# Weight-part buffers at eight offsets modulo 128 bytes, and activation parts of one stage 256 bytes apart

## What is computed

```python
def block(args):                       # peer_ffn, one block of tokens
    xb, ib, gb = args
    h = jax.nn.gelu(jnp.einsum('md,mkd->mk', xb, exp_u[ib]).astype(F32_2), approximate=False)
    coef = (gb * h).astype(xb.dtype)
    return jnp.einsum('mk,mkd->md', coef, exp_v[ib])
```

## The kernel before

| tensor | modulo 128 | modulo 1024 |
|---|---|---|
| `ring0` to `ring3`, `w_hi0` to `w_hi3`, `w_lo0` to `w_lo3` | 32 | 32 |
| `x_hi`, `x_lo` (every chunk of 256 columns) | 64 | 64 |
| `xn_hi`, `xn_lo`, `mixT_hi`, `mixT_lo`, `mixT1_*` | 64 | 448 |
| `mixT2_hi`, `mixT2_lo` | 32 | 672 |
| `mixT3_hi`, `mixT3_lo` | 64 | 576 |
| `hidden_hi`, `hidden_lo` (all four halves) | 64 | 832 |

## Time and profile before

### The profile page before, as it was taken

How to read it: one execution, slowest core, us unless ns; L and a number is a source line. 1 busy time by engine, 2 the same in 40 slices (tenths; PEclk the granted TensorE clock), 3 DMA queues, 4 the chain that set the end, 5 groups by cost and what they waited for, 6 DMA issues and landing times. The chain is left out here.

```text
span 2566.0 us, 62482 instructions
## 1 busy us (share of the span) xinstructions
PE 2430.2 (95%) x22900; PEld 2282.3 (89%) x22900; DVE 1673.7 (65%) x3915; ACT 1312.5 (51%) x2406; POOL 596.0 (23%) x494
## 2 busy tenths in 40 slices
PE   5998899999989999999999999879999999999998
PEld 3997667578978999999999999868999999999997
DVE  3032632636445966888998666665967888998665
ACT  3322643457345665555444554546665555445554
POOL 0335133157336930000000000637920000000000
PEclk9999999999999999999999999989999999999999
DMA  8554023034114554444444554424555444444552
GB/s 274 181 164 133 17 79 95 23 116 132 45 57 135 187 189 165 163 164 163 164 163 163 182 192 152 130 76 133 194 183 169 163 162 160 164 163 164 189 187 82
DMA packets 153876, 373.32 MB, mean 145 GB/s; under 512 B 8920, under 2 KB 102888, under 8 KB 137232
## 3 DMA queue, kind: packets, MB, share of 16 engines
q1 hardware_dynamic: 151232, 369.27, 42.9%
q10 hardware_dynamic: 2512, 2.24, 0.3%
HBM read 370.44 MB, written 1.05 MB: 145 GB/s over the span
## 5 line engine op out<-in xcount | busy, mean ns | idle before, releaser
L3012 ACT ACTIVATE w_hi<-ring 128x512 fp32r<-128x512 f32 x1024 | 643.1, 632 | 686.6 <-PE bank L3067 367.1
L3018 DVE TENSOR_TENSOR w_lo<-ring,w_hi 128x512 fp32r<-128x512 f32 x864 | 594.9, 691 | 310.2 <-ACT w_hi L3012 307.9
L3049 PE MATMUL bank<-x_hi,w_hi 128*128 128x256 f32 x2048 | 578.2, 282 | 3.8 <-DVE w_lo L3018 3.6
L3067 PE MATMUL bank<-hidden_hi,w_hi 128*128 128x256 f32 x2048 | 578.3, 282 | 0.0
L3067 PE MATMUL bank<-hidden_hi,w_lo 128*128 128x256 f32 x2048 | 574.3, 280 | 0.0
L3049 PE MATMUL bank<-x_hi,w_lo 128*128 128x256 f32 x2048 | 572.3, 279 | 0.0
L3049 PE MATMUL bank<-x_lo,w_hi 128*128 128x256 f32 x2048 | 571.9, 279 | 0.0
L3067 PE MATMUL bank<-hidden_lo,w_hi 128*128 128x256 f32 x2048 | 569.8, 278 | 0.0
L375 POOL TENSOR_TENSOR w_lo<-ring,w_hi 128x512 fp32r<-128x512 f32 (+3 forms) x260 | 337.0, 1313 | 653.5 <-ACT w_hi L366 645.2
L3049 PEld LDWEIGHTS bank<-x_hi,w_hi 128*128 128x128 f32 x2048 | 385.9, 188 | 4.8 <-ACT hidden L3142 4.0
L3049 PEld LDWEIGHTS bank<-x_lo,w_hi 128*128 128x128 f32 x2048 | 386.0, 188 | 0.0
(11 more groups left out here) (522 smaller groups left out, 4048.3 us busy)
## 6 DMA issues: line engine op xcount, KB each, us to landing
ring<-in_peer_uT SPq DMA_DIRECT2D x128, 1024.0 KB, 4.9
ring<-in_peer_v SPq DMA_DIRECT2D x128, 1024.0 KB, 4.8
ring<-in_even_w_in SPq DMA_DIRECT2D x26, 1024.0 KB, 5.6
ring<-in_ada_w SPq DMA_DIRECT2D x24, 1024.0 KB, 7.8
ring<-in_odd_w_in SPq DMA_DIRECT2D x12, 1024.0 KB, 5.4
ring<-in_even_w_out SPq DMA_DIRECT2D x8, 1024.0 KB, 5.4
ring<-in_odd_w_out SPq DMA_DIRECT2D x8, 1024.0 KB, 5.3
ring<-in_peer_w_q SPq DMA_DIRECT2D x8, 1024.0 KB, 5.2
```

Source lines behind the costliest of these rows:

```text
L3012: act.activation(k.hi[q][:, :], k.ring[slot][:, q * PART:q * PART + PART], ACT.Copy).then_inc(k.hi_ready, 1)
L3018: eng.tensor_tensor(k.lo[q][:, :], k.ring[slot][:, q * PART:q * PART + PART], k.hi[q][:, :].bitcast(F32), ALU.subtract).then_inc(k.lo_read ...
L3049: mm = pe.matmul(k.bank[s][:, j * T:j * T + T], a[q][:, w], b[:, cc, :], start=(cc == 0 and n == 0), stop=(cc == KC - 1 and n == 2))
L3067: mm = pe.matmul(out, a[q][:, w], b[:, j, :], start=first and cc % 2 == 0 and n == 0, stop=last and cc % 2 == 1 and n == 2, skip_group_che ...
```

## The change

The order of instructions and what each one waits for are the same on every engine; only addresses change. Each of the eight weight parts is now a view of 512 columns into a buffer of 768 (3072 bytes), and starts at an offset of its own. `hidden_hi` and `hidden_lo` get rows of 320 columns, of which 256 are used, and a spacer of 256 bytes ahead of them. The scratch for descriptors shrinks from 16384 to 1024 bytes, which makes room for this; no DMA of this kernel is issued from GpSimd.

```diff
+HI_AT, LO_AT = (0, 4, 2, 16), (20, 28, 6, 12)
...
-        self.hi = [self.sb(f"w_hi{i}", [P, PART], F32R) for i in range(PARTS)]
-        self.lo = [self.sb(f"w_lo{i}", [P, PART], F32R) for i in range(PARTS)]
+        self.hi = [self.sb(f"w_hi{i}", [P, PART + T], F32R)[:, HI_AT[i]:HI_AT[i] + PART] for i in range(PARTS)]
+        self.lo = [self.sb(f"w_lo{i}", [P, PART + T], F32R)[:, LO_AT[i]:LO_AT[i] + PART] for i in range(PARTS)]
...
-        self.hh = k.sb("hidden_hi", [P, 2, T], F32R)
-        self.hl = k.sb("hidden_lo", [P, 2, T], F32R)
+        k.sb("before_hidden_hi", [P, T // 4])
+        self.hh = k.sb("hidden_hi", [P, 2, T + T // 4], F32R)[:, :, 0:T]
+        self.hl = k.sb("hidden_lo", [P, 2, T + T // 4], F32R)[:, :, 0:T]
...
-    nc = bacc.Bacc("TRN2", target_bir_lowering=False, num_devices=1)
+    nc = bacc.Bacc("TRN2", target_bir_lowering=False, num_devices=1, dynamic_dma_scratch_size=1024)
```

## The result

The changed kernel takes 2576.87 us (median of 8, 2574.73 to 2579.49) against 2564.15 us for the kernel before in the same session (2560.69 to 2570.76): ratio 1.0045, 95% interval 1.0035 to 1.0055. It is slower by 11.5 us by the ratio (9 to 14 by the interval); the medians differ by 12.7. The profiled execution spans 2577.7 us, 11.7 more than before. The forecast was 8 us faster.

A forecast was written before the change was run, and what follows sets the result against it. TensorE's distance between matmul starts was taken as the bound. Excess over the floor, 5.1 + 0.8 + 4.5 + 2.6, summed to 13.0 us; 8 were taken, so 2561.7 − 8 = 2553.7 us, range 2546 to 2580.

The forecast's parts named there:

- What bounds the kernel: Whole kernel: TensorE is the bound, so the distance from one matmul's start to the next one's is what counts.
- Terms 1 and 2: All engines: no instruction, wait or DMA added, removed or moved; ScalarE's copies and VectorE's subtractions on shifted parts at no cost.
- The floor: TensorE: 116.67 ns per matmul is a property of a moving float32r operand of 256 columns at full clock, not a conflict.
- The rival under the floor: Experts: the 9% between bf16 and float32r is a conflict, the spread removes half, 49 us go: 2513; chance 0.05.
- The lock argument: Experts and tokens: eight relations break the slow pattern handed from matmul to matmul; down stage gains 5 us, tokens 2 to 3.
- Down stage: Experts' down stage: 4608 of 6144 matmuls run 1.1 ns over the floor; at most 5.1 us to win.
- Up stage: Experts' up stage: first layer at the floor; half of the second layer's gated matmuls may be 1.1 ns over, 0.8 us to win.
- the slower rival: Experts: new relations behave like the mixT rows, 118.6 ns, giving 2577 us, or 2599 at 120.0 ns for all; chance 0.30.
- First layer's tokens: First layer's token projections: 1344 matmuls at 120.0 ns, 4.5 us of excess, about half expected won, 2 to 3 us.
- The rival on the other side: Experts: giving up the old relation in seven of eight parts costs 17 us, less 2 for tokens: 2577 us; chance 0.30.
- The sign for the forecast: Down stage without gates: about 1545 matmuls in 180 us instead of 1531 would show the forecast right.
- the ports: TensorE: by the page's rule of separate ports the time would stay at 2562 us, within the nothing-measurable rival; chance 0.20.

The follow-up runs named there:

- the faster versions: The changed kernel with all parts at 96 bytes, 96 and 224 in turn, or 96, 224, 352 and 480, hidden activation as before: ratios 0.9845, 0.9812, 0.9809.
- the base run: The changed kernel with all eight part offsets at 0 and the hidden activation as before, keeping buffer pitch and small scratch: ratio 1.0001 to the kernel before.
- the kernel with the longer spacer: The kernel before with the spacer ahead of x_hi at 64 bytes instead of 32, moving every activation 32 bytes and no part: ratio 1.0012.

## Why the prediction was wrong, point by point

1. **What bounds the kernel** was right: the distance between TensorE's starts, nothing else. 11.3 of the 11.7 us of the loss are there, and TensorE's idle time did not change. The 39 to 49 us of the faster versions are there too, less 6 to 8 us by which TensorE's idle time grew (135.8 us before, 142 to 144 in them).
2. **Terms 1 and 2** (no instruction moves, ScalarE and VectorE at no cost) were right: 631 and 690 ns, and the base run at 1.0001.
3. **The floor** was the first step that failed. It was inferred from rows that all kept a relation other than 64. The 64-column loads and the 512 moving columns showed that a shorter or rarer load doesn't lower the distance; I took that as proof that the load has no part in it. The runs showed 113.3 ns with full loads at another relation. The rival under the floor, given 0.05, named a possible 49 us; 49 us came, but not from this change, which has no part in relation 64, and that the two numbers agree is luck. It took half of a 9% difference between bf16 and float32r, where the earlier trace rows give 7% (116.7 against 109.3 ns), so half of it would be 45 us.
4. **The lock argument** was the step that turned the sign: with eight relations the slow pattern would not survive, "because a matmul whose load is ready always runs at the floor". I held that a stretch hands its pattern on, and in the kernel before it does (one level per stretch). But a row of changing relations does not fall to the floor: the changed kernel has one level, 118.1 ns, in all 136 stretches, with no wait in them. Changing the relation inside a part doesn't free a row of its slow pattern; the run with high parts at 96 and low ones at 0 lost the low level by it. Nor does only a break change the level: with parts at 96 and 224 bytes in turn some rows dropped from 117.8 to 113.3 ns at a change of part. So the argument holds for those places, which share their relation modulo 128, and fails for the eight of this change.
5. **The terms.** Down stage: 5.1 us to win, 3.4 lost. Up stage: 0.8 to win, 7.4 lost. A stage that stands at the lowest distance of the trace has nothing to win and everything to lose, and the 8 us taken from the sum leave that side out; only the slower rival had it. First layer's tokens: 2 to 3 to win, 0.2 won.
6. **The rival on the other side** was right in place and sign, and near in size. It named the relation that was given up and its threshold (a mean over 117.6 ns; it became 118.1). It put the new relations at the mixT rows' 118.6, which was 0.5 too high: 17 us for the experts, and 10.8 came. It took 2 us off for the tokens that did not come. That its 2577 us is the median measured is luck in part: it stands on 2561.7 us for the kernel before, which had 2564.15 beside the changed one. Its mechanism, that giving up the relation costs, is borne out by the run with all parts at 64 bytes. A chance of 0.30 was too low for it: every row of the trace with another place was slower, and the forecast had no row of its own.
7. **The signs.** 1019 matmuls in 120 us of the up stage, fewer than 1031, was the sign of the slower rival. The sign for the forecast, about 1545 in the down window, seems met by the 1544 above, but only since small matmuls have slipped into the window. The gated slots did stop alternating, at 118.1 ns and not at the floor: that sign could not tell the two apart.
8. **On the ports**, the page "TensorE: Matmul & The Clock Gate" of the Trainium skill (section "Part 2: What happens when you issue a matmul") says that the weight load doesn't take read bandwidth from the running matmul. That sits badly with these runs of float32r operands: 113.3 to 123.4 ns in the down stage with nothing changed but the addresses of weight parts, which the experts' matmuls load and don't stream. They don't show that it is read bandwidth that is lost.

Open is what makes the levels: the runs show which there are, and that a break or, in one kernel, a change of part can bring another, not the mechanism inside the memory. The parts' new places are also where ScalarE and VectorE write. That these writes are needed for a new level is ruled out for one case: in the kernel with the longer spacer the parts stayed where they were, and its up stage has 113.3 ns, which the kernel before never had. Whether they have a share elsewhere was not tested. Open too is how the 118.1 ns of the changed kernel splits into relations (mean 117.9) and changes of relation within a part. By part it doesn't follow the mean at all: part 1 would have (2 × 117.6 + 118.7) / 3 = 118.0 ns and has 116.6, part 3 would have 118.3 and has 119.2.

## What to carry to other kernels

In this kernel, with back-to-back matmuls that each load new float32r weights, the place of the weight parts moved the distance between matmuls by up to 8% (113.3 against 123.3 ns). The start of the stationary operand relative to the moving one, modulo 128 bytes, was the first thing to look at, but not all of it: two kernels with relation 64 ran at 0.985 and 1.001 of the time. So try the multiples of 16 as one uniform shift, measure each, and only then spread anything. High and low parts of one buffer at different relations lost the gain in the one run that tried it; different buffers could differ by multiples of 128, and here that gained another 9 us. And a value that all rows of one layout share is no floor of the hardware: it may be the layout's.

## What was not expected of the hardware

- **Fixed levels.** A row of matmuls without a break runs at one of two or three exact distances (in the experts 113.3 or 117.8 ns at relation 64; 116.7 or 117.8 at 96), and a wait of 0.26 us can move it from one to the other. At offset 80 the level is itself a pattern: distances of about 117 and 130 ns in turn, mean 123.3.
- **GpSimd's subtraction is shorter on uneven starts.** Rows of the kernel before and of the one with all parts 8 bytes further (line, engine, operation, count, busy us, mean ns, idle):

```profile
L3018 POOL TENSOR_TENSOR w_lo<-ring,w_hi 128x512 fp32r<-128x512 f32 x160 | 203.0, 1299 | 33.5 <-ACT w_hi L3012 30.3
```

```profile
L3019 POOL TENSOR_TENSOR w_lo<-ring,w_hi 128x512 fp32r<-128x512 f32 x160 | 173.0, 1094 | 65.5 <-ACT w_hi L3013 65.0
```

  1094 ns again with all parts 24 bytes further, and 1297 with 48 or 1296 with 80. In the changed kernel, where one part in four starts unevenly, the mean is 1245 ns, and (3 × 1299 + 1094) / 4 is 1248. It was expected to be worse, if anything. GpSimd bounds nothing here, so it brought no time.
